# A two-block hybrid model: the rotated part of the latent attention's scores over 64 rows instead of 128, with the mask ahead of it

## The chip, the cores and the metric

One Trainium2 (trn2) chip, one of its cores. The metric is the device time of one execution in microseconds, as the median over several runs. The kernel is written in Bass, with an instruction stream by hand for each engine and semaphores between them: TensorE (PE; its weight loads are shown as PEld), VectorE (DVE), ScalarE (ACT), GpSimd (POOL) and SyncE (SP), which issues the DMAs.

## What is computed

Batch 1, 512 tokens, width 1024, float32. A first block (sparse attentions with compressed, selected and windowed keys, and an indexer) is followed by a second block of two layers and a last norm. Each of these two layers has a gated linear recurrence beside a multi-head latent attention (MLA), and a feed-forward part. The change lies in the MLA:

```python
def mla(q_down, kv_down, k_rope, cos, sin, ...):
    q = einsum('bsr,rhd->bshd', rms_norm(q_down), w_uq)          # 8 heads, 128 + 64
    q = concat([q[..., :128], apply_rope(q[..., 128:], ...)])
    kv = einsum('bsr,rhd->bshd', rms_norm(kv_down), w_ukv)       # 8 heads, 128 keys + 128 values
    k_pe = apply_rope(k_rope, cos, sin)                          # one for all heads, 64
    k = concat([kv[..., :128], broadcast(k_pe, 8 heads)])
    s = einsum('bqhd,bkhd->bhqk', q, k) * 192 ** -0.5
    s = where(key <= query, s, -inf);  p = softmax(s)
    return einsum('bhqk,bkhd->bqhd', p, kv[..., 128:])
```

So a head's score is the sum of a 128-wide product (its own keys) and a 64-wide product (rotated keys, the same for all heads), with a causal mask on it.

## The kernel before

Activations lie with features on the 128 partitions and the 512 tokens in the free dimension. All large weights come through one stream of 128x1024 slots (RAW, a ring of 7). ScalarE copies each into a rounded high half WH (L559, in `split_through`), GpSimd subtracts to get the low half WL (L469, in `pass_to`), and TensorE multiplies three times (L1660, L1661, L1662 in `mm3`): high by high, high by low, low by high. Each engine's program runs in a fixed order written out by hand; `pass_through` on GpSimd and `split_through` on ScalarE say up to which slot the splitting goes before the next other step. Eight PSUM banks are handed out in turn by `claim`, which waits for the last reader of the bank eight jobs ago; `full` signals that a bank is complete.

A layer of the second block goes through these steps: norm; the low-rank projections (kvq); the recurrence with its projections (xl, ga, lg); gates (ga, gb); then the MLA. Its latents are transposed (`turn`, L1739), the fourth transpose giving the rotated keys of 64 rows. ScalarE moves these into KPE (L828, L829). The query's rotated part for all heads is computed (L1661 and its neighbours with WH, CQH), rotated on VectorE and transposed into QRT [128, 4, 512], where plane i holds head 2i in rows 0 to 63 and head 2i+1 in rows 64 to 127. V2 holds all heads' values. `head_qk` computes QN and KN, 128 rows each, for a head, in two buffers.

KPE is [128, 2, 512] in the kernel before: plane 0 has the rotated keys in rows 0 to 63 and zeros in rows 64 to 127, plane 1 zeros in rows 0 to 63 and the keys in rows 64 to 127. GpSimd sets the zeros in each layer (L539, L540), behind the splits up to slot `hd` 0 and behind the wait for the last gated YA (L1497), since the tile lies over memory used by the recurrence; it then goes on with the splits up to `hd` 3. A product of a plane of QRT over 128 rows with plane `hd % 2` of KPE thus counts the rows of one head.

The score stage is a list of 32 units per layer (8 heads, and 4 query tiles of 128 each), `UNITS2`, of which unit u has n = 128 (qt + 1) key columns. For unit u TensorE waits for QN and KN, claims a bank, and issues three matmuls into it: QN by KN (L2027), QRT by KPE (L2029), and the identity by the causal mask in bfloat16 on the last 128 columns (L2031), which ends the group and signals `full`. Matmuls in float32 (L2027, L2029, L2038, L2047) are two passes of the hardware each with its own weight load, so the trace has twice as many records; a transpose of 128x128 is a single pass. VectorE takes the maximum (L1541), ScalarE the exponential (L863), VectorE the reciprocal and the normalising (L1548, L1550), TensorE transposes the probabilities of unit u - 3 (L2038, T_LAG = 3), ScalarE or, for query tile 3, VectorE moves them out (L851), and once per head TensorE multiplies by the values (L2047), at u = 7, 11 and so on. After the second unit of heads 1 to 6 TensorE computes QN and KN of the next head. Behind the stage come the output projection (o2), the norm and the feed-forward part, dense three-fold matmuls.

Rows of 64 are used elsewhere in the kernel too, each time with the operands sliced to a half of the partitions: in the index logits of the first block (L1797, tiles QIT and KIT, heads in turn on rows 0 to 63 and 64 to 127) and in its compressed scores (L1877, tiles KCT and QNT). Before the index logits stands a projection (L1660 to L1662), behind them transposes (L1739); before the compressed scores stands a product of probabilities and values (L1927), behind them the attention's scores (L1902).

Of the kernel before, what the change touches and what calls it, by code (L numbers as in the profile page):

```python
# [34 lines left out]
ACT = mybir.ActivationFunctionType  # L35
F32 = mybir.dt.float32
# [5 lines left out]
P = 128  # L42
# [173 lines left out]
def program(nc, a, known):  # L216

    note = {}
    with ExitStack() as ctx:
# [45 lines left out]
        def w(name, shape, dt, kb):  # L265

            return at(name, shape, dt, W0 + kb * KB)
# [55 lines left out]
        XCL = w("XCL", [P, 2, S], F32R, 84)  # L323
        V2 = w("V2", [P, NT, D], F32, 32)
        QRT = w("QRT", [P, 4, S], F32, 48)
        KPE = w("KPE", [P, 2, S], F32, 66)
        QN = w("QN", [P, 2, S], F32, 58)
        KN = w("KN", [P, 2, S], F32, 62)
        P2 = at("P2", [P, RING, S], F32, 16 * KB)
# [24 lines left out]
        def mark(name, *key, by=1):  # L354

            count[name] += by
            note[(name,) + key] = count[name]
            return by

        def value(*key):  # L360

            if known and key not in known:
                raise KeyError(key)
            return known.get(key, 1)
# [85 lines left out]
        def _(pool):  # L450
# [83 lines left out]
            for layer in range(LAYERS):  # L534

                pass_through(("gb", layer, KD - 1))
                pool.wait_ge(sem["ya_gated"], value("ya_gated", layer, KD - 1))
                pool.wait_ge(sem["passed"], max(1, count["passed"]))
                nc.gpsimd.memset(KPE[DH:P, 0, :], 0.0)  # L539
                nc.gpsimd.memset(KPE[0:DH, 1, :], 0.0).then_inc(sem["pool_set"], mark("pool_set", "kpe", layer))  # L540
                pool.wait_ge(sem["pool_set"], value("pool_set", "kpe", layer))
                pass_through(("hd", layer, 3))
                add_squares(f"f{layer}", SQT, SQ2, lambda k: ("o2", layer, k))
                add_squares(next_norm(layer), SQT, SQ2, lambda k: fo_slot(layer, 1, k))
# [3 lines left out]
        def _(act):  # L548
# [210 lines left out]
            for layer in range(LAYERS):  # L759
# [60 lines left out]
                for i in range(3):  # L820
# [4 lines left out]
                        sem["c_hi"], mark("c_hi", L, i))  # L825
                act.wait_ge(sem["full"], value("full", "tc2", L, 3))
                b = bank_of("tc2", L, 3)
                nc.scalar.activation(KPE[0:DH, 0, :], b[0:DH, :], ACT.Copy)  # L828
                nc.scalar.activation(KPE[DH:P, 1, :], b[0:DH, :], ACT.Copy).then_inc(  # L829
                    sem["read_act"], mark("read_act", "tc2", L, 3))  # L830
                split_through(("uqr", L))
                for tt in range(NT):
# [784 lines left out]
        def _(pe):  # L1617
# [34 lines left out]
            def full(ins, *key):  # L1652
                return ins.then_inc(sem["full"], mark("full", *key))
# [290 lines left out]
            for layer in range(LAYERS):  # L1944
# [71 lines left out]
                for u in range(nU + O_LAG):  # L2016
                    if u < nU:
                        hd, qt = UNITS2[u]
                        n = (qt + 1) * P
                        if u == 0:  # L2020
                            pe.wait_ge(sem["pool_set"], value("pool_set", "kpe", L))
                            pe.wait_ge(sem["read_act"], value("read_act", "tq", L, 3))
                            pe.wait_ge(sem["read_act"], value("read_act", "tc2", L, 3))
                        pe.wait_ge(sem["read_act"], value("read_act", "qn", L, hd))
                        pe.wait_ge(sem["read_dve"], value("read_dve", "kn", L, hd))
                        b = claim("s", 2 + L, u)
                        nc.tensor.matmul(b[:, 0:n], QN[:, hd % 2, qt * P:(qt + 1) * P], KN[:, hd % 2, 0:n],  # L2027
                                         start=True, stop=False)
                        nc.tensor.matmul(b[:, 0:n], QRT[:, hd // 2, qt * P:(qt + 1) * P], KPE[:, hd % 2, 0:n],  # L2029
                                         start=False, stop=False)  # L2030
                        full(nc.tensor.matmul(b[:, n - P:n], identb[:], causal[:], start=False, stop=True),  # L2031
                             "s", 2 + L, u)
                    v = u - T_LAG
                    if 0 <= v < nU:
                        pe.wait_ge(sem["p_norm"], value("p_norm", 2 + L, v))
# [181 lines left out]
```

## Time and profile before

| | us |
|---|---|
| median of 3 runs | 1863.71 (1862.32 to 1866.21) |
| the profiled execution | 1857.34 |
| its span, first to last instruction | 1855.5 |
| TensorE busy in the span | 1774.3 (96%) |
| VectorE, ScalarE, GpSimd busy | 973.9, 715.0, 730.1 |
| mean granted TensorE clock | 0.985 |
| score stage of the first layer | 635.3 to 711.7 |
| score stage of the second layer | 1348.8 to 1425.7 |

The profiled execution is one of its own and the rows are of that one. Its span is what its rows add up to; what lies around the span is 1.84 us. A row of the timeline gives the start, the length, the engine, the line and the tiles written and read; the shapes are rows x columns of the weights and then the moving operand, and several equal instructions in a row are merged into one, marked x2 and so on, whose length goes from the first start to the last end. Matmuls are pipelined, so a pass starts before the one ahead has ended; the lengths of passes include this overlap, and the ends are modelled. In brackets stands the idle time before, and what ended it; "issue" is a wait for nothing that the profile shows.

### The profile page before, as it was taken

What the parts mean: (1) busy time and instruction counts of PE and PEld (TensorE: products, weight loads), DVE (VectorE), ACT (ScalarE), POOL (GpSimd) and SP (SyncE); (2) the same over time, 40 slices, a digit from 0 to 9 for tenths busy, and PEclk for the clock granted to TensorE, in tenths of its full rate; (3) what the DMA queues carried; (4) which work ended last, traced back from release to release, by engine and by line L of the source; (5) the groups of instructions that cost most, each with busy time, mean ns of one, the idle gap of its engine ahead of it and who ended that gap; (6) DMA issues with size and microseconds to landing.
All of it is one profiled execution on the core that took longest, in us unless ns stands there. A gap on an engine that the chain in (4) does not pass through costs nothing. (4 is left out here: it accounts for less than half of the span.)

```text
span 1855.5 us, 23527 instructions
## 1 busy us (share of the span) xinstructions
PE 1774.3 (96%) x8439; PEld 1436.7 (77%) x8445; DVE 973.9 (52%) x1707; ACT 715.0 (39%) x1234; POOL 730.1 (39%) x317
## 2 busy tenths in 40 slices
PE   6999999989999999899999999999999999999997
PEld 5877777777887766788888887887866788888886
DVE  6999688583679767633333321669966221101112
ACT  5434555523474642332212222365454232222321
POOL 2434111246445302455455545354511544344442
PEclk8999999999999999999999999999999999999998
DMA  6234010053332204455555532232310223232211
GB/s 229 92 102 137 24 35 24 24 194 124 102 113 91 66 26 145 162 204 182 181 181 198 188 136 91 69 125 80 114 34 23 80 91 103 91 101 97 98 57 46
DMA packets 56345, 197.66 MB, mean 107 GB/s; under 512 B 6961, under 2 KB 7985, under 8 KB 56242
## 3 DMA queue, kind: packets, MB, share of 16 engines
q1 hardware_dynamic: 56242, 196.26, 31.4%
q8 instruction: 68, 1.11, 0.3%
q14 instruction: 35, 0.29, 0.1%
HBM read 194.14 MB, written 2.10 MB: 106 GB/s over the span
## 5 line engine op out<-in xcount | busy, mean ns | idle before, releaser
L469 POOL TENSOR_TENSOR WL<-RAW,WH 128x1024 fp32r<-128x1024 f32 x256 | 652.7, 2555 | 924.9 <-ACT WH L559 654.3
L1660 PE MATMUL bank<-HH,WH 128*128 128x512 f32 x1120 | 439.4, 392 | 12.4 <-POOL WL L469 8.6
L1662 PE MATMUL bank<-HH,WL 128*128 128x512 f32 x1120 | 437.7, 391 | 0.0
L1661 PE MATMUL bank<-HL,WH 128*128 128x512 f32 x1120 | 437.4, 391 | 0.0
L559 ACT ACTIVATE WH<-RAW 128x1024 fp32r<-128x1024 f32 x260 | 271.6, 1052 | 267.0 <-PE bank L1662 221.6
L1660 PEld LDWEIGHTS bank<-HH,WH 128*128 128x128 f32 x1120 | 211.3, 189 | 58.8 <-issue 7.7
L1662 PEld LDWEIGHTS bank<-HH,WL 128*128 128x128 f32 x1120 | 211.3, 189 | 44.3
L1661 PEld LDWEIGHTS bank<-HL,WH 128*128 128x128 f32 x1120 | 211.6, 189 | 43.7
L1593 DVE TENSOR_TENSOR HF<-SILU,bank 128x512 f32<-128x512 f32 x44 | 30.3, 688 | 326.0 <-PE bank L1662 323.0
L1660 PE MATMUL bank<-HDH,WH 128*128 128x512 f32 x352 | 137.2, 390 | 0.0
L1662 PE MATMUL bank<-HDH,WL 128*128 128x512 f32 x352 | 137.0, 389 | 0.0
L1661 PE MATMUL bank<-HDL,WH 128*128 128x512 f32 x352 | 136.9, 389 | 0.0
L1660 PE MATMUL bank<-WH,HH 128*128 128x512 f32 (+2 forms) x288 | 111.9, 389 | 22.8 <-DVE WL L1110 10.6
L1604 DVE SCALAR_TENSOR_TENSOR X<-bank,mod,X 128x512 f32<-128x512 f32 x32 | 24.0, 751 | 199.7 <-PE bank L1662 199.7
L929 DVE SCALAR_TENSOR_TENSOR ACC<-RAW,vec,ACC 128x1024 f32<-128x1024 f32 x77 | 113.5, 1475 | 5.1 <-DMA RAW<-in_stream 0.8
L1661 PE MATMUL bank<-WL,HH 128*128 128x512 f32 (+2 forms) x288 | 110.7, 384 | 0.0
L1662 PE MATMUL bank<-WH,HL 128*128 128x512 f32 (+2 forms) x288 | 110.6, 384 | 0.0
L891 ACT ACTIVATE HDH<-HF 128x512 fp32r<-128x512 f32 x44 | 27.8, 631 | 195.1 <-DVE HF L1593 195.1
L1660 PEld LDWEIGHTS bank<-WH,HH 128*128 128x128 f32 x288 | 55.1, 191 | 33.3 <-DVE WL L1110 10.6
L567 ACT ACTIVATE SILU<-bank 128x512 f32<-128x512 f32 x44 | 26.3, 597 | 139.4 <-PE bank L1662 139.4
L1662 PEld LDWEIGHTS bank<-HDH,WL 128*128 128x128 f32 x352 | 66.1, 188 | 13.8
L1660 PEld LDWEIGHTS bank<-HDH,WH 128*128 128x128 f32 x352 | 66.1, 188 | 13.6
(355 smaller groups left out, 2829.8 us busy)
## 6 DMA issues: line engine op xcount, KB each, us to landing
RAW<-in_stream SPq DMA_DIRECT2D x364, 512.0 KB, 3.4
X<-in_xt SPq DMA_DIRECT2D x4, 512.0 KB, 8.1
out_t<-YA SPq DMA_DIRECT2D x8, 256.0 KB, 2.2
ACC<-in_pos SPq DMA_DIRECT2D x1, 256.0 KB
gains<-in_gains SPq DMA_DIRECT2D x1, 224.0 KB
CS<-in_cs SPq DMA_DIRECT2D x1, 128.0 KB
cw<-in_cw SPq DMA_DIRECT2D x1, 128.0 KB
par<-in_par SPq DMA_DIRECT2D x1, 115.0 KB
```

The lines of the kernel that those rows point to most:

```text
L469: nc.gpsimd.tensor_tensor(lo(k)[:], raw(k)[:], hi(k)[:].bitcast(F32), ALU.subtract).then_inc(sem["passed"], mark("passed", *k))
L559: nc.scalar.activation(hi(k)[:], raw(k)[:], ACT.Copy).then_inc(sem["w_hi"], mark("w_hi", *k))
L567: return nc.scalar.activation(dst, b[0:dst.shape[0], 0:n], func, **kw).then_inc(sem["read_act"], mark("read_act", *key))
L891: nc.scalar.activation(HDH[:, f % FH, :], HF[:, f % 2, :], ACT.Copy).then_inc(sem["hid_hi"], mark("hid_hi", L, f))
L929: ins = V.scalar_tensor_tensor(out=acc, in0=raw(k)[:], scalar=c, in1=acc, op0=ALU.mult, op1=ALU.add)
L1593: V.tensor_tensor(HF[:, f % 2, :], SILU[:, f % 2, :], b[:], ALU.mult).then_inc(sem["hid"], mark("hid", L, f))
L1604: ins = V.scalar_tensor_tensor(out=X[:, n, :], in0=b[:], scalar=mod[:, L, 5 * KD + n:5 * KD + n + 1], in1=X[:, n, :], op0=ALU.mult, op1=AL ...
L1660: nc.tensor.matmul(out, A[0], B[0], start=first, stop=False)
L1661: nc.tensor.matmul(out, A[0], B[1], start=False, stop=False)
L1662: return nc.tensor.matmul(out, A[1], B[0], start=False, stop=last)
```

## The change

KPE becomes one plane [128, 512] with the rotated keys twice, in rows 0 to 63 and in rows 64 to 127. Both memsets of GpSimd go, with the three waits around them and TensorE's wait for them. ScalarE's two copies write the halves of the one plane. In each unit the mask is the second matmul of the group; the rotated product is the last, signals `full`, and reads 64 rows of QRT and of KPE: rows 0 to 63 for even heads, 64 to 127 for odd ones.

```diff
--- before.py
+++ after.py
@@ -323,7 +323,7 @@
         XCL = w("XCL", [P, 2, S], F32R, 84)
         V2 = w("V2", [P, NT, D], F32, 32)
         QRT = w("QRT", [P, 4, S], F32, 48)
-        KPE = w("KPE", [P, 2, S], F32, 66)
+        KPE = w("KPE", [P, S], F32, 66)
         QN = w("QN", [P, 2, S], F32, 58)
         KN = w("KN", [P, 2, S], F32, 62)
         P2 = at("P2", [P, RING, S], F32, 16 * KB)
@@ -534,11 +534,6 @@
             for layer in range(LAYERS):
 
                 pass_through(("gb", layer, KD - 1))
-                pool.wait_ge(sem["ya_gated"], value("ya_gated", layer, KD - 1))
-                pool.wait_ge(sem["passed"], max(1, count["passed"]))
-                nc.gpsimd.memset(KPE[DH:P, 0, :], 0.0)
-                nc.gpsimd.memset(KPE[0:DH, 1, :], 0.0).then_inc(sem["pool_set"], mark("pool_set", "kpe", layer))
-                pool.wait_ge(sem["pool_set"], value("pool_set", "kpe", layer))
                 pass_through(("hd", layer, 3))
                 add_squares(f"f{layer}", SQT, SQ2, lambda k: ("o2", layer, k))
                 add_squares(next_norm(layer), SQT, SQ2, lambda k: fo_slot(layer, 1, k))
@@ -825,8 +820,8 @@
                         sem["c_hi"], mark("c_hi", L, i))
                 act.wait_ge(sem["full"], value("full", "tc2", L, 3))
                 b = bank_of("tc2", L, 3)
-                nc.scalar.activation(KPE[0:DH, 0, :], b[0:DH, :], ACT.Copy)
-                nc.scalar.activation(KPE[DH:P, 1, :], b[0:DH, :], ACT.Copy).then_inc(
+                nc.scalar.activation(KPE[0:DH, :], b[0:DH, :], ACT.Copy)
+                nc.scalar.activation(KPE[DH:P, :], b[0:DH, :], ACT.Copy).then_inc(
                     sem["read_act"], mark("read_act", "tc2", L, 3))
                 split_through(("uqr", L))
                 for tt in range(NT):
@@ -2018,7 +2013,6 @@
                         hd, qt = UNITS2[u]
                         n = (qt + 1) * P
                         if u == 0:
-                            pe.wait_ge(sem["pool_set"], value("pool_set", "kpe", L))
                             pe.wait_ge(sem["read_act"], value("read_act", "tq", L, 3))
                             pe.wait_ge(sem["read_act"], value("read_act", "tc2", L, 3))
                         pe.wait_ge(sem["read_act"], value("read_act", "qn", L, hd))
@@ -2026,10 +2020,10 @@
                         b = claim("s", 2 + L, u)
                         nc.tensor.matmul(b[:, 0:n], QN[:, hd % 2, qt * P:(qt + 1) * P], KN[:, hd % 2, 0:n],
                                          start=True, stop=False)
-                        nc.tensor.matmul(b[:, 0:n], QRT[:, hd // 2, qt * P:(qt + 1) * P], KPE[:, hd % 2, 0:n],
-                                         start=False, stop=False)
-                        full(nc.tensor.matmul(b[:, n - P:n], identb[:], causal[:], start=False, stop=True),
-                             "s", 2 + L, u)
+                        nc.tensor.matmul(b[:, n - P:n], identb[:], causal[:], start=False, stop=False)
+                        r = slice(DH * (hd % 2), DH * (hd % 2) + DH)
+                        full(nc.tensor.matmul(b[:, 0:n], QRT[r, hd // 2, qt * P:(qt + 1) * P], KPE[r, 0:n],
+                                              start=False, stop=True), "s", 2 + L, u)
                     v = u - T_LAG
                     if 0 <= v < nU:
                         pe.wait_ge(sem["p_norm"], value("p_norm", 2 + L, v))
```

## Rows read from the trace of the kernel before

**Rows 1.** The page: part 1, and the chain by engine.

```profile
PE 1774.3 (96%) x8439; PEld 1436.7 (77%) x8445; DVE 973.9 (52%) x1707; ACT 715.0 (39%) x1234; POOL 730.1 (39%) x317
...
PE 43%; DVE 4%; issue 1%; ACT 0%; POOL 0%; DVEq 0%; ACTq 0%
```

**Rows 2.** Stretches: us; PE, PEld, DVE, ACT, POOL busy; clock; DMA share; GB/s.

```profile
635.30:711.70 76.40, 73.69 (x350) 50.17 (x350) 53.22 (x131) 38.81 (x106) 7.08 (x3) 1.00 0.07 21
1424.00:1445.00 21.00, 19.91 (x80) 15.63 (x81) 5.08 (x8) 5.60 (x9) 7.54 (x4) 0.92 0.15 51
```

**Rows 3.** Waits of TensorE in the second layer's stage, 1348.5 to 1450 us.

```profile
PE bank L2038 <- DVE P L1550: 1.6, 1, 1.6
...
PE bank L2047 <- issue: 0.6, 2, 0.3
```

**Rows 4.** By tile and line: durations min/median/max in ns, first and last start, forms.

```profile
L2029 PE MATMUL bank<-KPE,QRT x128: 275/432/593, 635.6 to 1419.2; 128*128 128x128 f32 x32, 128*128 128x256 f32 x32, 128*128 128x384 f32 x32, 128*128 128x512 f32 x32
...
L2031 PE MATMUL bank<-causal,identb x64: 219/219/219, 635.8 to 1419.6; 128*128 128x128 bf16 x64
...
L2038 PE MATMUL bank<-ident,P x160: 272/273/328, 640.1 to 1424.6; 128*128 128x128 f32 x160
```

**Rows 5.** Timeline of one unit of the stage (query tile 1): start, length, engine, line.

```profile
650.85 0.60 PE L2027 MATMUL bank<-KN,QN 128*128 128x256 f32 x2
...
651.28 0.59 PE L2029 MATMUL bank<-KPE,QRT 128*128 128x256 f32 x2
...
651.72 0.22 PE L2031 MATMUL bank<-causal,identb 128*128 128x128 bf16 x1
651.72 0.31 PEld L2038 LDWEIGHTS bank<-ident,P 128*128 128x128 f32 x3
651.77 0.50 PE L2038 MATMUL bank<-ident,P 128*128 128x128 f32 x3
```

**Rows 6.** By tile: the index matmuls of the first block.

```profile
L1797 PE MATMUL bank<-KIT,QIT x24: 376/482/589, 86.5 to 112.6; 64*128 64x256 f32 x8, 64*128 64x384 f32 x8, 64*128 64x512 f32 x8
```

**Rows 7.** Timeline, 128 rows to 64, before the index matmuls.

```profile
85.97 0.39 PE L1661 MATMUL bank<-WL,HH 128*128 128x512 f32 x1
...
86.19 0.39 PE L1662 MATMUL bank<-WH,HL 128*128 128x512 f32 x1
...
86.51 0.19 PEld L1797 LDWEIGHTS bank<-KIT,QIT 64*128 64x128 f32 x2 [0.35 <-issue]
86.51 0.49 PE L1797 MATMUL bank<-KIT,QIT 64*128 64x256 f32 x2
```

**Rows 8.** Timeline, 64 rows to 128, behind them.

```profile
86.83 0.81 PE L1797 MATMUL bank<-KIT,QIT 64*128 64x256 f32 x6
...
87.58 0.42 PEld L1739 LDWEIGHTS bank<-ident,G 128*128 128x128 f32 x4 [0.33 <-ACT G L567]
87.58 0.66 PE L1739 MATMUL bank<-ident,G 128*128 128x128 f32 x4
```

**Rows 9.** Timeline, first block's attention, around its compressed scores (two windows).

```profile
251.36 0.66 PE L1927 MATMUL bank<-G,PT 128*128 128x64 f32 x4 [0.59 <-DVE PT L1326]
...
251.95 0.29 PEld L1877 LDWEIGHTS bank<-KCT,QNT 64*128 64x128 f32 x2
...
253.00 0.50 PE L1877 MATMUL bank<-KCT,QNT 64*128 64x32 f32 x3
253.43 0.49 PE L1902 MATMUL bank<-KT,QNT 128*128 128x128 f32 x2
```

**Rows 10.** Timeline, TensorE at the end of the first layer's stage.

```profile
707.92 0.71 PE L2038 MATMUL bank<-ident,P 128*128 128x128 f32 x5
710.18 0.65 PE L2038 MATMUL bank<-ident,P 128*128 128x128 f32 x4 [1.56 <-DVE P L1550]
```

**Rows 11.** Timeline, GpSimd behind the memsets.

```profile
614.42 0.52 POOL L540 MEMSET KPE<- 64x512 f32 x1
619.29 2.40 POOL L469 TENSOR_TENSOR WL<-RAW,WH 128x1024 fp32r<-128x1024 f32 x1 [4.35 <-ACT WH L559]
```

## The prediction

> **What bounds the kernel.** I read the page first [rows 1]. TensorE is busy 96% of the span, and it is the first item of the chain that ended last; no other engine is above 52%. A microsecond added to TensorE's own stream is therefore a microsecond of the kernel, unless the stage around it makes TensorE wait. So the question is what the latent-attention stage looks like. Its two passes (one per layer) are about 76 us each [rows 2]: TensorE busy 73.69 us of 76.40 at clock 1.00 (2.4 GHz), VectorE 50.17, ScalarE 53.22, GpSimd 7.08, DMA share 0.07. It is a TensorE stage. What TensorE waits for in it [rows 3] is small: per layer 1.6 us once, at the end of the stage, and two waits of 0.3 us (in the first layer one). Everything after the stage is dense TensorE work, so nothing further down takes the time back.
>
> The change touches one matmul of each unit, L2029 [rows 4]: two hardware passes per matmul, 128 passes in all, 64 units (8 heads x 4 query tiles x 2 layers). One whole unit is in [rows 5]: two KN passes, two KPE passes, the mask (0.219 long [rows 4]), then the transposes of the unit three back. The reader should see how dense it is. A 256-column pass follows the one before by 0.215 us (650.85 to 651.28 for two), the mask occupies 0.05 us (651.72 to 651.77), and each weight load starts with the *previous* pass and is hidden behind it, as the transposes' load at 651.72 does with the mask. A single 256-column pass is shown as 0.38 us long, so about 0.165 us of a pass's length is tail that the next pass overlaps.
>
> **Part 1: half the rows.** Does a 64-row pass take less? The index matmuls are the same form (64 rows, 128 weight columns, f32) [rows 6]: a 512-column pass took 589 ns at most, against 593 for KPE's over 128 rows [rows 4]. So it is priced at zero gain. They do show a gain of another kind: two heads on different row halves start together (two loads and two passes at 86.51 [rows 7], six passes within 0.81 us from 86.83 [rows 8]). The changed unit has no partner: one 64-row matmul stands between 128-row work, and its two passes use the same rows, which in the index stage follow one another (first passes 86.51 [rows 7], second 86.83).
>
> **Part 2: going from 128 rows to 64 and back.** This unit does it twice, and the kernel before has such places elsewhere. Going in [rows 7]: the last 128-row pass starts at 86.19, and the next load should start with it; it starts at 86.51, when the pass's stream (0.22, the pace of 85.97 to 86.19) has been over for 0.09 to 0.10 us, that is 0.07 us before the pass's shown end (86.19 + 0.39). Then the load is bare: the second pass follows the first by 0.32 us (86.51 to 86.83) instead of 0.215, so 0.105 more. Going out [rows 8]: six passes end at 87.64, the next load starts at 87.58, again 0.06 before the end; four transposes then last 0.66 us, where four in an unbroken stream are 0.273 + 3 x 0.108 = 0.60 (a single one 0.273 [rows 4], five unbroken 0.71 [rows 10]), so the bare load costs 0.055 in front of transposes. Attention of the first block repeats it [rows 9]: load at 251.95 where the last 128-row pass ends at 252.02, load at 253.43 where the last 64-row pass ends at 253.50, and two 128-column f32 passes in 0.49 instead of 0.275 + 0.107 = 0.38, so 0.105 for the bare load. Same gap after streams of very different length.
>
> Priced into the unit. In: the mask (0.219 long, stream 0.054) now stands before KPE, so KPE's load starts at 0.219 - 0.07 = 0.15 after the mask's start, which is 0.095 later than the stream would let it, plus 0.105 bare load = **0.20**. Out: the load of the transposes starts 0.095 after KPE's stream instead of under it, plus 0.055, less the 0.01 that is bare there now (three transposes behind the mask last 0.50 [rows 5], against 0.273 + 2 x 0.108 = 0.49) = **0.14**. The three first units of a layer have f32 scores behind instead of transposes, bare 0.105, but about 0.06 is bare today behind the short mask, so the same 0.14. Sum 0.34 x 64 = **21.8 us**.
> After a bf16 mask no row shows the entry. Bounds: nothing (an unbroken stream), and 0.165 + 0.107 = 0.27 (the whole tail, then the load). I take the 0.20, since all the changes shown have the same gap.
>
> The Trainium skill, in "TensorEngine Tiling (Array Packing)", Tiling Modes, Key Properties, says that changing the tiling mode, not just the tile, drains TensorE; the trace agrees, with its 0.09 us, and the page has no figure.
>
> **Part 3: order.** The mask's move costs nothing of itself: its load is hidden behind the last KN pass as now behind the last KPE pass. The "score full" signal now comes from a KPE pass: 0.05 + 0.20 + 0.165 = 0.42 us after four streams instead of 0.22, so VectorE's maximum starts 0.20 later. Behind it are exponent, reciprocal and normalising, and TensorE's transposes of that unit, three units later. TensorE itself is later by 3 x 0.34 there, so that chain gains slack, except at the end of a layer.
>
> **Part 4: what takes some back.** The last unit of a layer is followed by a wait of 1.56 us on its own chain [rows 10]; the chain starts 0.20 later, TensorE is 0.34 later, so 0.14 vanishes, 0.3 in two layers. The short waits of 0.3 before L2047 (one in the first layer, two in the second [rows 3]) stand behind a full unit and vanish: 0.9. Together 1.2.
>
> **Part 5: GpSimd.** Two memsets of 0.52 us per layer and their waits go. Behind them in GpSimd's queue is the subtraction of the next weight, which then waits 4.35 us for ScalarE's split [rows 11]; so they are hidden with 3 us to spare, and removing them gives 0. TensorE's wait for them at the first score was over 20 us old. ScalarE still writes KPE twice with the same two copies; 0. No DMA is moved.
>
> **Sum.** 21.8 - 1.2 = +20.6 us. On the profiled execution (1857.34 us, span 1855.5 with 1.8 around it) that gives 1877.9. It lies 6.4 us under the median of the three runs, 1863.71; against the median: **1884.3**.
>
> **Rivals.**
> *A, the whole tail is paid (slower).* Each change of rows waits for the full 0.165 instead of 0.095: 0.07 x 128 = 9 us more, 1893. For: no row has a bf16 pass before a change. Against: four places read, all the same. Chance 0.07.
> *B, the gap belongs to something else (not slower).* All the loads at the changes shown are the first of a new job and carry a semaphore wait. If the gap were the wait's, KPE's load, which follows the mask inside a job, would have none, and the transposes' load has its wait today at no cost (651.72, with the mask's start [rows 5]); with both changes at zero the time stays 1863.7. It decides if the entry is under 0.01 us. Against: that very load shows that a wait that is over costs nothing. Chance 0.04.
> *C, half the rows, half the time (faster).* KPE's streams sum to 64 units: 16 x 2 x (0.107 + 0.213 + 0.32 + 0.427) = 34 us; halved, 17 us less; with the changes free, 1847. Against: no lone passes run so [rows 6, 8]. Chance 0.02. The Trainium skill's page "TensorEngine Tiling (Array Packing)", Theoretical Speedup, promises up to 2x for a small dimension of 64; the pairs of the index stage agree, and those are two matmuls on two halves.
> *D, a clock loss.* TensorE's stream share falls in the stage, and after the waits at the end of the second layer's the clock is 0.92 over 21 us [rows 2], which is 0.08 x 21 = 1.7 us lost to the half level (1.2 GHz). Whether such a loss falls in more or fewer places moves the time by 1.7 us each; this is width, not a case.
>
> **Numbers.** Forecast 0.87. Its own width: 0.03 us on each of 128 changes is 4, clock losses 3, runs 2: 1877 to 1891. The range takes one microsecond or two beyond at each side: 1875 to 1892; it leaves out A, B and C, 13 in 100. About 0.2% (3.7 us) is what a measurement of this kernel tells from no change. Faster 0.03 (C and a piece of B), same 0.04, slower 0.93.
>
> **What would show it.** L2029's passes read 64x128..64x512 with the same durations; its first load starts 0.15 after the mask's start, first-to-second pass 0.1 above the stream; the transposes' load 0.095 after the last KPE stream. Both stages are about 10 us longer, all else equal; the waits of 0.3 before L2047 are gone, the 1.56 is 0.14 shorter. Wrong if the KPE load starts with the mask, or if the stage grows by over 14 us or under 6.

## The result, and the profile after

| | before | changed |
|---|---|---|
| median, us (runs) | 1863.49 (4) | 1892.03 (4), 1880.14 to 1894.84 |
| the same kernels again, beside the experiments | 1861.92 (17) | 1889.54 (6), 1881.96 to 1900.69 |
| mean granted clock, in those runs | 0.981 to 0.985 | 0.972 to 0.984 |

The ratio is 1.0139, 95% interval 1.0093 to 1.0185: slower, as forecast. The forecast was 1884.3 with a range of 1875 to 1892, so the first median, 1892.03, lies on the range's upper edge; two of its four runs (1894.38, 1894.84) lie above it. And the changed kernel spreads over 20 us where the kernel before spreads over 9. TensorE's clock, below, has a large part in both.

The page of the changed kernel (parts 1 and 2, the chain by engine), against [rows 1]:

```profile
PE 1814.3 (96%) x8439; PEld 1444.9 (76%) x8445; DVE 974.7 (52%) x1707; ACT 717.4 (38%) x1234; POOL 727.2 (38%) x313
...
PEclk8999999999999999999999999999989999999998
...
PE 43%; DVE 4%; issue 1%; ACT 1%; POOL 0%; DVEq 0%; ACTq 0%
```

As many matmuls and loads as before, four GpSimd instructions fewer, and TensorE 40 us longer busy: the same passes, further apart, in part at a lower clock. The two stages by stretch, from the first KN pass to the first pass of the output projection (columns as in [rows 2]). In the kernel before:

```profile
635.30:713.90 78.60, 75.85 (x359) 51.57 (x359) 53.22 (x131) 38.81 (x106) 7.08 (x3) 1.00 0.06 21
1348.80:1429.20 80.40, 77.36 (x358) 52.36 (x359) 54.01 (x131) 38.81 (x106) 9.43 (x4) 0.98 0.08 27
```

In the changed kernel, and behind them two parts at half level:

```profile
640.50:732.90 92.40, 88.83 (x359) 51.16 (x359) 54.38 (x131) 39.61 (x106) 7.01 (x3) 0.97 0.05 18
1367.40:1465.80 98.40, 95.94 (x359) 54.37 (x359) 52.33 (x131) 39.71 (x106) 9.38 (x4) 0.90 0.07 22
1369.60:1386.70 17.10, 17.10 (x38) 8.95 (x38) 5.25 (x16) 6.87 (x19) 2.52 (x2) 0.50 0.00 0
727.90:734.70 6.80, 6.09 (x12) 3.94 (x13) 1.99 (x3) 0.00 (x1) 0.00 (x0) 0.50 0.00 0
```

The stages are 13.8 and 18.0 us longer. The third row is the surprise: 17.1 us of the second stage ran at half level (0.50, that is 1.2 GHz), with TensorE shown 100% busy. At full level that work takes half, so about 8.5 us are the clock's. The first stage lost some 2.5 us in its last 5.0. The two stages hold 31.8 of the 37 us between the two profiles; the other 5.2 lie ahead of the first stage, which starts at 640.5 instead of 635.3. They are not the change's: in a later profile of the kernel before, with fillers in the stages alone, the first stage starts at 640.1.

Now a unit of the changed kernel, the counterpart of [rows 5] (timeline, query tile 1):

```profile
694.18 0.60 PE L2021 MATMUL bank<-KN,QN 128*128 128x256 f32 x2
...
694.62 0.22 PE L2023 MATMUL bank<-causal,identb 128*128 128x128 bf16 x1
...
694.76 0.29 PEld L2025 LDWEIGHTS bank<-KPE,QRT 64*128 64x128 f32 x2 [0.26 <-issue]
694.76 0.70 PE L2025 MATMUL bank<-KPE,QRT 64*128 64x256 f32 x2
...
695.39 0.31 PEld L2032 LDWEIGHTS bank<-ident,P 128*128 128x128 f32 x3 [0.33 <-issue]
```

And the three transposes behind it, in the timeline of TensorE alone:

```profile
695.39 0.55 PE L2032 MATMUL bank<-ident,P 128*128 128x128 f32 x3
```

KPE's load starts 0.14 after the mask's start (694.62 to 694.76), the two passes last 0.70 where they were 0.59, the transposes' load starts at 695.39, 0.07 before the end of the passes (694.76 + 0.70), and three transposes last 0.55 instead of 0.50. KN's start to the transposes' start: 1.21 instead of 0.92 (650.85 to 651.77). So 0.29 + 0.05 = 0.34 per unit, the predicted price, in the predicted places.

TensorE's waits in the first stage (us in total, times, longest), against [rows 3] and [rows 10]:

```profile
PE bank L2041 <- ACT PT L846: 2.0, 2, 1.1
PE bank L2032 <- DVE P L1545: 1.6, 1, 1.6
PE bank L2021 <- ACT QRT L562: 0.8, 1, 0.8
```

The 1.6 before the last transposes stayed. One wait is new: of the two before a value product, 0.9 was there before, 1.1 was not. In this profile it comes in the first layer only; in the second profile of the changed kernel, which has both stages at full level, it comes in both (1.09 and 1.08, behind normalising instructions of 2.50 and 2.49 us). The timeline around it:

```profile
651.62 4.66 POOL L469 TENSOR_TENSOR WL<-RAW,WH 128x1024 fp32r<-128x1024 f32 x2 [19.14 <-ACT WH L554]
...
653.93 2.50 DVE L1545 TENSOR_SCALAR P<-P,coef 128x256 f32<-128x256 f32 x1
...
656.35 0.68 DVE L1555 COPY PT<-bank 128x512 f32<-128x512 f32 x1
657.13 1.10 PE L2041 MATMUL bank<-PT,V 128*128 128x512 f32 x2 [1.09 <-ACT PT L846]
```

A normalising instruction of 0.35 us took 2.50. It starts where the second of two GpSimd subtractions starts (651.62 + 2.3) and ends 0.15 after it (656.43 against 656.28), and VectorE's move of PT, for which the value product waits, stands behind it. The view names ScalarE's PT, but that move had begun at 656.08; the late one is VectorE's.

### The profile page after: what moved, and what is told of

The parts are those of the page before. It is cut to its first block and busy times, and to the rows that moved or that the text cites. A ratio compares the mean times of both kernels' runs of the same rounds, so it can differ in the third digit from the quotient of the medians.

```text
span 1892.5 us, 23517 instructions
## 1 busy us (share of the span) xinstructions
PE 1814.3 (96%) x8439; PEld 1444.9 (76%) x8445; DVE 974.7 (52%) x1707; ACT 717.4 (38%) x1234; POOL 727.2 (38%) x313
## 5 line engine op out<-in xcount | busy, mean ns | idle before, releaser
L1657 PEld LDWEIGHTS bank<-HDH,WL 128*128 128x128 f32 x352 | 66.1, 188 | 13.8
L1656 PEld LDWEIGHTS bank<-HDL,WH 128*128 128x128 f32 x352 | 66.1, 188 | 13.7
```

The costliest lines, as they stand in the source:

```text
L1656: nc.tensor.matmul(out, A[0], B[1], start=False, stop=False)
L1657: return nc.tensor.matmul(out, A[1], B[0], start=False, stop=last)
```

## The experiments

A run's time holds a varying share of half clock. To compare kernels in spite of it, I use, beside the medians, the span times the mean clock: in it a microsecond at half level counts half. It is rough, since waits don't get shorter with the clock, but the six runs of the changed kernel, 19 us apart in time, lie within 4 us of their median in it. Each ratio is to the kernel before as measured beside that kernel: its median was 1861.92 in the first group (the change again, order alone, mask last, two units), 1862.77 in the second (one plane, values later, heads in pairs, changed with waits filled) and 1862.47 in the third (the other three), and its span x clock 1826.9, 1826.3 and 1826.9. Medians of different groups are compared across those 0.85 us. The clock column is the mean over the runs; a "step" in the pair experiments is what TensorE issues for two units together.

| kernel | median, us | ratio to before, 95% interval | clock | span x clock, median | stages in the profile, us (clock) |
|---|---|---|---|---|---|
| before | 1861.92 (17 runs) | | 0.982 | 1826.9 | 78.6 (1.00), 80.4 (0.98) |
| changed, again | 1889.54 | 1.0155, 1.0129 to 1.0182 | 0.979 | 1847.2 | 90.2 (1.00), 90.2 (1.00) |
| order alone | 1866.11 | 1.002, 1.0009 to 1.0031 | 0.981 | 1827.7 | 79.8 (1.00), 81.5 (0.98) |
| 64 rows, mask last | 1884.13 | 1.0123, 1.0101 to 1.0144 | 0.981 | 1847.4 | 90.8 (0.98), 90.4 (0.99) |
| one plane, 128 rows | 1862.69 | 0.9997, 0.9988 to 1.0007 | 0.982 | 1826.2 | 79.8 (0.98), 80.7 (0.98) |
| two units together | 1894.34 | 1.0164, 1.0145 to 1.0183 | 0.979 | 1852.0 | 95.9 (0.96), 95.3 (0.96) |
| and values later | 1874.00 | 1.0059, 1.0043 to 1.0075 | 0.982 | 1837.5 | 86.2 (0.99), 85.0 (1.00) |
| heads in pairs | **1854.73** | 0.9962, 0.9949 to 0.9975 | 0.983 | 1821.4 | 76.7 (1.00), 77.1 (1.00) |
| pairs, four units | 1867.74 | 1.0033, 1.0021 to 1.0044 | 0.982 | 1832.2 | 83.1 (0.98), 81.5 (1.00) |
| changed, waits filled | 1880.57 | 1.0099, 1.0084 to 1.0115 | 0.983 | 1847.3 | 90.2 (1.00), 90.2 (1.00) |
| before, waits filled | 1861.21 | 0.9994, 0.9983 to 1.0005 | 0.983 | 1826.3 | 78.6 (1.00), 79.1 (1.00) |
| changed, splits later | 1885.63 | 1.0121, 1.0087 to 1.0154 | 0.980 | 1847.0 | 90.6 (0.98), 95.2 (0.93) |

### The change again

> The changed kernel again, unaltered, five rounds, for its clock. Theory C (about 21 us are gaps, the rest is half-clock stretches that come and go with the start of the stage): over the runs, time falls on a line with the clock: span x (1 - clock) taken off each run leaves +16 to +22 us over the kernel before treated alike, and runs with clock 0.984 take about 1880. Rival: the gaps alone give +28 to +30, at equal clocks too.

Borne out. "Theory C" is the reading of the half-level stretches as an addition to the gaps that comes and goes. Over the six runs span x clock has a median 20.3 us above that of before, against a forecast of +20.6; the two runs at clock 0.983 took 1882, the one at 0.972 took 1901. This profile happens to have both stages at clock 1.00, and so shows the gaps alone:

```profile
640.80:731.00 90.20, 86.65 (x358) 49.98 (x359) 54.39 (x131) 39.62 (x106) 7.01 (x3) 1.00 0.05 18
1364.30:1454.50 90.20, 86.62 (x357) 49.94 (x358) 54.38 (x131) 39.61 (x106) 9.36 (x4) 1.00 0.07 24
```

Against 78.6, the first stage has 11.6 more: 32 x 0.34 = 10.9, plus the new wait of 1.1, less what waits gave back. The second has 9.8 more than 80.4, of which before had lost about 1.3 to the clock; in the later profile of the kernel before with fillers, it is at full level:

```profile
1353.50:1432.60 79.10, 78.48 (x370) 52.64 (x370) 53.95 (x131) 38.86 (x106) 9.42 (x4) 1.00 0.08 27
```

So the second has 11.1 more, and the two together 22.7: the 21.8 of the gaps, two new waits of 1.1, less the three short ones of 0.3. That is 2 us over the 20.6 of the sum.

### The order alone

```diff
@@ kernel before
                         nc.tensor.matmul(b[:, 0:n], QN[...], KN[...], start=True, stop=False)
-                        nc.tensor.matmul(b[:, 0:n], QRT[...], KPE[:, hd % 2, 0:n], start=False, stop=False)
-                        full(nc.tensor.matmul(b[:, n - P:n], identb[:], causal[:], start=False, stop=True), "s", 2 + L, u)
+                        nc.tensor.matmul(b[:, n - P:n], identb[:], causal[:], start=False, stop=False)
+                        full(nc.tensor.matmul(b[:, 0:n], QRT[...], KPE[:, hd % 2, 0:n], start=False, stop=True), "s", 2 + L, u)
```

> The kernel before with only the order changed: QN by KN, mask, QRT by the padded KPE over 128 rows; memsets kept. Theory R (a change of rows costs, the order does not): within 2 us of the kernel before, first KPE load with the mask's start minus nothing bare, stage about 78.6 us. Rival O (it is the long last matmul before the signal, or the mask ahead of it): most of the 21 us appear here, each stage about 10 us longer.

Rival O is out: of the 28 us of the changed kernel's median, 4.2 appear here (1866.11 against 1861.92). But it is not within the 2 us expected, and the difference is instructive: 0.2% slower, each stage about 1.2 us longer. The timeline of a unit:

```profile
694.77 0.60 PE L2027 MATMUL bank<-KN,QN 128*128 128x256 f32 x2
695.21 0.22 PE L2029 MATMUL bank<-causal,identb 128*128 128x128 bf16 x1
695.26 0.65 PE L2030 MATMUL bank<-KPE,QRT 128*128 128x256 f32 x2
695.75 0.49 PE L2037 MATMUL bank<-ident,P 128*128 128x128 f32 x3
```

KPE's passes last 0.65 instead of 0.59. The mask's stream (0.05) is too short to hide the f32 load that now follows it; in the kernel before a transpose's load followed it, which needs less. So the move costs 0.055 per unit, less the 0.01 that is no longer bare before the transposes: 1.4 us per layer, of which 1.2 show in the stage.

### 64 rows, but the mask last

```diff
@@ changed kernel
-                        nc.tensor.matmul(b[:, n - P:n], identb[:], causal[:], start=False, stop=False)
-                        r = slice(DH * (hd % 2), DH * (hd % 2) + DH)
-                        full(nc.tensor.matmul(b[:, 0:n], QRT[r, ...], KPE[r, 0:n], start=False, stop=True), "s", 2 + L, u)
+                        r = slice(DH * (hd % 2), DH * (hd % 2) + DH)
+                        nc.tensor.matmul(b[:, 0:n], QRT[r, ...], KPE[r, 0:n], start=False, stop=False)
+                        full(nc.tensor.matmul(b[:, n - P:n], identb[:], causal[:], start=False, stop=True), "s", 2 + L, u)
```

> The changed kernel (64 rows, one plane, no memsets) with the mask last, as in the kernel before. Two changes of rows per unit remain. Theory R: entry 0.20 us as before; on the way out the gap of 0.095 stands before the mask, whose load is bare (bf16), then 0.01 before the transposes: 0.32 to 0.36 per unit, so a stage at full clock is longer than before by 10 to 12 us, total +20 us plus lost clock. Rival O: back to the time of the kernel before.

```profile
692.03 0.60 PE L2021 MATMUL bank<-KN,QN 128*128 128x256 f32 x2
692.55 0.70 PE L2024 MATMUL bank<-KPE,QRT 64*128 64x256 f32 x2
693.18 0.23 PE L2026 MATMUL bank<-causal,identb 128*128 128x128 bf16 x1
693.25 0.50 PE L2033 MATMUL bank<-ident,P 128*128 128x128 f32 x3
```

As theory R has it, the cost goes with the rows in the main, not with the order: most of it stays with the old order. KPE's passes start 0.08 before KN's end here and 0.08 before the mask's end in the changed kernel; the gap is the same behind an f32 pass and behind a bf16 one. KN to the transposes' start takes 1.22, as with the mask first (1.21), but the three transposes behind last 0.50 instead of 0.55, since their load is hidden by the mask as in the kernel before. So the unit costs 0.30 more than before, a little under the 0.32 to 0.36 expected, and the order is worth 0.04 to 0.05 per unit here as in the experiment above. That makes some 3 us in all, which these four runs cannot tell: their span x clock goes from 1844.9 to 1849.9, its median within 0.2 us of the changed kernel's.

### One plane, all 128 rows

```diff
@@ changed kernel
-                        full(nc.tensor.matmul(b[:, 0:n], QRT[r, ...], KPE[r, 0:n], start=False, stop=True), "s", 2 + L, u)
+                        nc.tensor.matmul(b[:, 0:n], QRT[:, ...], KPE[:, 0:n], start=False, stop=False)
+                        full(nc.tensor.matmul(b[:, n - P:n], identb[:], causal[:], start=False, stop=True), "s", 2 + L, u)
```

> The changed kernel's storage (one plane, no memsets, no waits for them) with the product over all 128 rows and the mask last. It leaves out the separation of the two heads of a plane: each score gets the rotated part of both. Theory R: no change of rows is left, so the time is the kernel before's within 2 us, and the memsets were worth 0. Rival: the memsets or their waits had a cost or a use, and the time differs by more than 3 us from before at equal clock.

0.9997 (0.9988 to 1.0007), and span x clock equal to 0.1 us: the memsets, their waits and the second plane were worth nothing, either way, to within the 2 us of the interval.

### Two units together

The 64-row products of two successive units of one head follow each other, on the same rows, in two banks; everything else keeps its place.

```diff
@@ changed kernel, TensorE
-                    if u < nU:
+                    if u < nU and u % 2 == 0:
...
+                        for x in (u, u + 1):
...
+                            b = claim("s", 2 + L, x)
+                            bs.append(b)
+                            nc.tensor.matmul(b[:, 0:n], QN[...], KN[...], start=True, stop=False)
+                            nc.tensor.matmul(b[:, n - P:n], identb[:], causal[:], start=False, stop=False)
+                        for b, x in zip(bs, (u, u + 1)):
...
+                            full(nc.tensor.matmul(b[:, 0:n], QRT[r, ...], KPE[r, 0:n], start=False, stop=True), "s", 2 + L, x)
```

> The changed kernel with two successive units of a head issued together: KN and mask of both, then both 64-row products (same row half). One entry and one exit per two units. Theory R: 32 x 0.34 = 11 us over the kernel before at full clock, 10 to 11 less than the changed kernel, and the second product's load is hidden behind the first's pass. Rival (each 64-row product pays by itself, whoever its neighbour is): no gain over the changed kernel. If the stage's clock loss comes from the gaps, the granted clock in the stages is nearer to 1.00 than in the changed kernel.

A miss: not 10 us faster than the changed kernel but 5 slower. The clock is not nearer to 1.00 either: it was 0.96 in both stages, though at the first stage's start, where there are half as many changes now, it was 1.00 (640.7 to 650); the low parts are 650 to 662 (0.86) and 725 to 736.6 (0.79), which hold the first and the last waits before value products. The timeline of a pair with 384 and 512 columns:

```profile
689.90 0.22 PE L2026 MATMUL bank<-causal,identb 128*128 128x128 bf16 x1
690.05 1.77 PE L2031 MATMUL bank<-KPE,QRT 64*128 64x384 f32 x4
...
693.30 1.10 PE L2047 MATMUL bank<-PT,V 128*128 128x512 f32 x2 [0.79 <-ACT PT L846]
```

And TensorE's waits before the value products in the first stage:

```profile
PE bank L2047 <- ACT PT L846: 5.6, 7, 0.9
PE bank L2047 <- issue: 1.7, 1, 1.7
```

The price per change held: four passes of 384 and 512 columns in 1.77 are 2 x 0.32 + 2 x 0.427 of streams, 0.107 of one bare load and 0.165 of tail, so the second product entered for nothing. But a cover was lost. Before, a whole unit of 512 columns stood between the transposes of a head's last tile and the product that reads them; here both units stand ahead of the transposes, and TensorE waits for the move from the bank, eight times in the stage.

### And the value product one step later

```diff
@@ two units together
-                    if u >= 7 and (u - 7) % 4 == 0:
-                        hd = (u - 7) // 4
+                    if u >= 8 and (u - 8) % 4 == 0:
+                        hd = (u - 8) // 4
```

VectorE and ScalarE take its result one step later too.

> The run with two successive units together, with the product with the values one step later (behind the next two units' scores instead of right behind the transposes), and its readers shifted with it. Theory R with a lost cover: the eight waits of 1.0 us per layer before the value product vanish, so about 14 to 16 us less than with two units together, a stage of about 84.5 us at full clock, half of the changed kernel's excess. Rival (the long groups themselves starve the chain): the waits come back before the transposes, and the stage stays at 90 us or over.

Borne out in the main: 20 us less than without it by the medians and 14.5 by span x clock, against 14 to 16 expected. Of the eight waits before a value product two are left in each layer, 0.6 and, before the last product, 2.8, where nothing is left to cover it. In the stage at clock 1.00, 85.0 us is 5.2 less than the changed kernel's 90.2, for 16 entries and exits fewer (16 x 0.34 = 5.4), with about the same sum of waits (4.2 against 4.4). Half the changes, half the excess.

### Heads in pairs, on both halves

The unit list takes two heads per query tile, so that the two 64-row products of a step lie on rows 0 to 63 and 64 to 127.

```diff
@@ changed kernel, its core
-UNITS2 = [(h, qt) for h in range(HEADS) for qt in range(NT)]
+UNITS2 = [(2 * p + i, qt) for p in range(HEADS // 2) for qt in range(NT) for i in range(2)]
...
+        QNB = at("QNB", [P, 2, S], F32, 37 * KB)
+        KNB = at("KNB", [P, 2, S], F32, 41 * KB)
...
+                    if u % 8 == 0 and u < 24:
+                        head_qk(2 * p + 2)
+                    turn_unit(u - 3)
+                    if u >= 10 and u % 8 == 2:
+                        value_head(2 * p - 2)
+                        value_head(2 * p - 1)
+                    turn_unit(u - 2)
+                    if u % 8 == 2 and u < 24:
+                        head_qk(2 * p + 3)
```

The scores of a step are issued as in the two experiments before; `turn_unit` holds the transposes, `value_head` the product with the values. The first head's value product stands in front of the second's, to cover the move that the second waits for.

> Heads in pairs: the unit list goes over two heads for each query tile, and the 64-row products of the two heads, on rows 0 to 63 and 64 to 127, are issued together; QN and KN have four buffers (the two new ones over the query's raw rotated part, dead by then). Theory R, with the index matmuls' overlap: the KPE streams take half, 8.5 us per layer less; 16 entries and exits per layer cost 5.4; so each stage 3 us shorter than in the kernel before, if no new wait appears, and 13 shorter than in the changed one: about 1855 to 1862. Rival (the pair does not overlap when four passes follow a mask, or the longer distance to the transposes makes waits): stage 84 us or more, time over 1870.

This is the fastest kernel of the study: 1854.73 us, 0.4% under the kernel before (interval 0.25 to 0.51%), 1.8% under the changed one. A step of 512 columns:

```profile
670.26 1.08 PE L2061 MATMUL bank<-KNB,QNB 128*128 128x512 f32 x2
671.18 0.22 PE L2063 MATMUL bank<-causal,identb 128*128 128x128 bf16 x1
671.33 1.13 PE L2068 MATMUL bank<-KPE,QRT 64*128 64x512 f32 x4
```

Four passes of 512 columns last 1.13 us, as long as two of them do in the changed kernel (0.693 for the longest one plus 0.427). That is the overlap that the index matmuls had shown [rows 7, 8], and only with it does computing on half the rows pay in these runs: per layer 8.5 us of streams less, 16 x 0.34 = 5.4 of changes more.

```profile
639.50:716.20 76.70, 74.76 (x359) 46.05 (x359) 54.93 (x130) 37.78 (x106) 7.08 (x3) 1.00 0.06 21
1349.60:1426.70 77.10, 74.89 (x357) 46.03 (x358) 56.29 (x130) 37.68 (x106) 9.41 (x4) 1.00 0.09 28
```

1.9 and 2.0 us under 78.6 and the 79.1 of a second stage without clock loss; 3 were expected. The first row of the step shows a cost that the sum had left out: the second KN product starts behind the first's mask, which hides too little of an f32 load, so its two passes take 1.08 where they take 1.02 in the kernel before; 16 such places make 0.9 us per layer. TensorE's listed waits went down by as much (2.8 against 3.6 in the first stage), so about one microsecond per layer stays unexplained. The order of the heads is part of this experiment too, and the same order with 128 padded rows was not measured; that the four passes take the time of two is what the timeline shows directly.

### Four units of a pair in one group

```diff
@@ heads in pairs
-                    if u < nU:
+                    if u < nU and u % 8 != 2:
+                        group = tuple(range(u, u + (4 if u % 8 == 0 else 2)))
...
```

`head_qk` of the next pair stands behind the transposes here, and the readers of its results two units later.

> Heads in pairs, with the first two query tiles of a pair of heads in one group: four 64-row products together, 12 entries and exits per layer instead of 16. Theory R: 4 x 0.34 = 1.4 us per layer less, 2.7 in all, about 1852, if the value products and transposes keep their cover. Rival (lost cover, as with two units together): a wait of 0.5 to 1 us per pair of heads before the transposes or value products, so no gain or up to 4 us slower.

The rival won, and by more than it had asked: 1867.74 us, 13 us slower than heads in pairs, where at most 4 had been expected. The largest three of the first stage's waits:

```profile
PE bank L2032 <- ACT QNB L576: 2.8, 2, 1.5
PE bank L2032 <- DVE P L1560: 1.5, 3, 0.6
PE bank L2032 <- ACT QN L576: 1.4, 1, 1.4
```

1.4 to 1.5 us before a transpose (L2032), three times per layer, released by ScalarE's move of QN or QNB: by the code, the bank that the transposes claim still holds the next head's queries, which ScalarE moves out two units later than before. 1.4 us of changes less, 4.2 of these waits more; the stages are 6.4 us (at clock 0.98) and 4.4 us longer. That the grouping itself would pay with the banks in another order was not tried.

### The changed kernel with its waits filled

```diff
@@ changed kernel, TensorE
+                def fill(i, n):
+                    b = claim("warm", f"s{L}", i)
+                    for _ in range(n):
+                        nc.tensor.matmul(b[:], identb[:], keep[:], start=True, stop=True)
...
+                            fill(0, 4)
...
+                            fill(1, 7)
...
+                            fill(2, 4)
```

They stand before the first unit, before the last unit's transposes and before the last value product.

> The changed kernel with filler matmuls (bf16, 512 columns, result unused) in three waits of TensorE in each layer's stage: 4 before the first unit, 7 before the last unit's transposes, 4 before the last value product. Theory C (the half-clock stretches at the start and end of the stage come from these waits together with the gaps): clock 1.00 in both stages, span x (1 - clock) smaller by 3 to 15 us, the time of most runs near 1880 and less spread than 1882 to 1901. Rival: the stretches come whatever is in the waits; same times as the changed kernel, or up to 1 us more.

All four runs took 1880.42 to 1881.38 us; the changed kernel without fillers 1880 to 1901 in ten, measured beside other kernels. The stages are as long as in the profile of the changed kernel at clock 1.00, and span x clock is the same to 0.1 us. So the fillers take no work away, they keep the clock: 9 us of the changed kernel's median went with them. The three waits were filled together, so the runs do not show which of them matters. The profile of the first section points at the first: the half level set in at 1369.6, behind the 0.84 before the first unit and the first two units, which have few columns and four changes of rows:

```profile
1367.37 0.49 PE L2021 MATMUL bank<-KN,QN 128*128 128x128 f32 x2 [0.84 <-ACT QRT L562]
...
1368.94 0.70 PE L2025 MATMUL bank<-KPE,QRT 64*128 64x256 f32 x2
1369.57 1.59 PE L2021 MATMUL bank<-KN,QN 128*128 128x384 f32 x2
```

Two 384-column passes took 1.59 there, 0.81 at full level. It stayed at the half level through units whose changes of rows go on, and rose at 1386.7, 4.9 us after the dense matmuls of `head_qk` had begun (1381.83). The changed kernel with later splits, below, has another such stretch in its profile, 13.7 us from 1367.3 in a second stage that starts at 1365.5. But the other profile of the changed kernel has the same wait and the same first units at full level. That the gaps held the clock down is argued from these stretches, not shown, and why it falls in some executions and not in others stays open.

### The kernel before with its waits filled

> The kernel before with the same filler matmuls in TensorE's three waits of each layer's stage. Theory C: the kernel before loses only 2.7 us of half clock there, behind the second stage, so at most 1 to 2 us come off, and this shows how much of the filled changed kernel's gain was its own loss. Rival (fillers help anywhere): 4 us or more faster than the kernel before.

The same fillers in the kernel before give 0.9994 (0.9983 to 1.0005): it had almost nothing to lose there. Its ten runs still go from 1856.1 to 1864.8, so the fillers do not remove the spread that comes from outside the stages, and four runs within 1 us, as of the filled changed kernel, are in part luck. Heads in pairs with fillers was not measured.

### The changed kernel with later splits

```diff
@@ changed kernel, ScalarE
-                        if qt == 1 and 1 <= h < HEADS - 1:
-                            split_through(("hd", L, (h + 1) // 2))
+                        if qt == 3 and 1 <= h < HEADS - 1:
+                            split_through(("hd", L, (h + 1) // 2))
+                        if qt == 1 and 1 <= h < HEADS - 1:
...
```

> The changed kernel with ScalarE's splits for the next head's weights two units later (query tile 3 instead of 1), and with them GpSimd's subtractions. Theory P (VectorE's normalising took 2.5 us instead of 0.36 because a GpSimd subtraction began with it and both want the same access to SBUF; TensorE's wait of 1.1 us before the first value product is its echo): the normalising of that unit is back at 0.4 us and the wait before the first value product is under 0.3, in both layers where it was; another VectorE instruction may meet the subtraction instead. Rival: the wait belongs to the first value product itself and stays.

VectorE at the place where the 2.50 had been:

```profile
652.49 0.35 DVE L1546 TENSOR_SCALAR P<-P,coef 128x256 f32<-128x256 f32 x1
652.76 0.68 DVE L1556 COPY PT<-bank 128x512 f32<-128x512 f32 x1
```

And TensorE:

```profile
654.28 0.33 PE L2033 MATMUL bank<-ident,P 128*128 128x128 f32 x1
654.44 2.32 PE L2042 MATMUL bank<-PT,V 128*128 128x512 f32 x8
```

0.35 instead of 2.50, and no wait before the first value product, in either layer: the long normalising and TensorE's wait go with the time of the subtractions, as theory P has it. As expected, the subtractions meet other instructions now (the longest normalising took 1.70), where no wait of TensorE in the stage's list comes from it. By the times of the whole kernel nothing can be told: 1885.63 us and span x clock 1847.0, against 1889.54 and 1847.2. The Trainium skill, in "SBUF — State Buffer", Terms, says that VectorE and GpSimd share a pair of ports as an exclusive lock, held for a whole instruction. The traces agree: the normalising instructions of 2.50, 1.19 (in the kernel before) and 1.70 us began while a subtraction ran or started, and ended 0.15, 0.15 and 0.1 us after its end.

## Why the prediction was right, point by point

- **Half the rows, zero gain** (part 1): right. In the changed kernel a unit's two passes, less the bare load, take what they took; only with a partner on the other half, as in heads in pairs, do two products take the time of one.
- **Entry 0.20, exit 0.14** (part 2): right, in place and size: 0.34 per unit in the timeline; with two units together and the value product later, half of it. The open point, the entry behind a bf16 mask, came out at the value taken (load 0.14 to 0.15 after the mask's start). Rival A, the whole tail, is out, since both loads start 0.07 to 0.08 before the shown end of what is in front.
- **The order costs nothing** (part 3): wrong as a statement, though not in the sum. The move alone costs about 0.05 us per unit, since the mask hides less of an f32 load than of a transpose's. In the changed kernel the load at the entry is bare in either order, but the one at the exit is the transposes' (0.055) instead of the mask's (about 0.01); part 2 had priced the exit by the order that the kernel has, so the total came out. With the mask last the unit costs 0.30.
- **What is taken back, 1.2 us** (part 4): wrong. The short waits before L2047 (0.83 in sum) went, but their reason was another: in the kernel before they stood behind normalising instructions of 1.2 us that had met a GpSimd subtraction, and a unit being longer shifted the meeting. It shifted into a worse one, a new wait of 1.1, in one layer or in both. The 1.56 at the end of the stage was to be 0.14 shorter and stayed 1.56. With both stages at full level the waits give about 1.2 us on top, where 1.2 were to come off.
- **GpSimd's memsets, 0** (part 5): right, 0.9997 without them, to within 2 us.
- **Rival B** (the gap belongs to the wait): out; KPE's load waits for nothing by semaphore and has the gap. **Rival C**: out for a lone product.
- **Rival D, the clock**: the term that was mis-sized. I gave it 3 us of width and placed it behind the stages. The sum itself, 20.6, lies between what span x clock shows (20.3) and what the two stages show at full level (22.7). What the median has beyond it, 1889.5 to 1892 against 1884, is half-level time. The one long stretch, 17.1 us, cost 8.5; the median of the runs lies 9.0 above the filled kernel's. The sign that I had set for being wrong, a stage longer by over 14 us, was met by the second stage (18.0), through the clock alone: at full level it is 11.1. In the row of [rows 2] for the second stage's end I had the sign of it (0.92), and took it for noise around a fixed mean; it was a mean that the change itself moves. That the first median still fell on the edge of the range is in part luck: the mechanism gives 1884, and nothing in the prediction gives the other 5 to 8 us.

## What to carry to other kernels

In this kernel, half the rows were only worth taking where two products on the two halves of TensorE stood side by side; a lone one took the same time, and each change between 128 and 64 rows cost the 0.095 us of gap plus the next load, bare (0.055 for a transpose, 0.105 for f32 weights). Group such products, and when grouping moves work, look for what it had covered: the wait that comes in its place can cost more than the changes saved. Where gaps are added to TensorE's stream, look at the granted clock of the stretch with the shortest passes and at the spread over several runs, not at one profile.

## What the runs showed of the hardware that was not expected

- TensorE at half level stayed there for 17.1 us in which the profile shows it 100% busy; with 15 filler matmuls per stage, in waits of 0.8 to 1.6 us, four runs lay within 1 us at 1880.6, where ten without had spread over 20.
- A VectorE instruction of 0.35 us took 2.50 us where it began together with a GpSimd subtraction of 2.3 us, and the meeting moved with the length of TensorE's units.
- A weight load behind a bf16 pass of 128 columns is bare by about 0.055 us if it is an f32 load, by 0.01 if it is a transpose's.
- Heads in pairs: four 64-row passes of 512 columns, on two halves, in 1.13 us, in the middle of 128-row work.
